# Weights alone in one DMA queue, x in five pieces issued by ScalarE, first chunk in three passes

## The reference, cut to what matters

```
def even_layer(h, norm_g, w_in, ...):
    p = rms_norm(h, norm_g) @ w_in
    ...
    return jnp.concatenate([o_a, o_b, o_m], axis=-1) @ w_out

def reference(x, mem, ...):
    h = x
    for layer in range(DEPTH):
        h = h + (even_layer if layer % 2 == 0 else odd_layer)(h, ...)
    return h
```

## Time and profile before

| | |
|---|---|
| median of 3 runs | 1442.42 us (1442.23 to 1443.27) |
| the profiled execution | 1443.31 us |
| its span in the profile | 1441.6 us |
| TensorE busy | 98% of the span |
| VectorE, ScalarE, GpSimd busy | 62%, 53%, 9% |
| bytes moved | 236.42 MB, 164 GB/s over the span |

### The profile page before, as it was taken

One profiled execution on the slowest core, in us unless ns is written; L12 is line 12 of the kernel. 1 busy time (PEld: TensorE's weight loads), 2 busy tenths in 40 slices (PEclk: granted clock), 3 DMA queues, 4 the chain that ended last, 5 costly groups with the idle time before them and its releaser, 6 DMA issues.

```text
span 1441.6 us, 18169 instructions
## 1 busy us (share of the span) xinstructions
PE 1413.8 (98%) x6869; PEld 1174.9 (82%) x6869; DVE 890.5 (62%) x1289; ACT 759.6 (53%) x1179; POOL 125.3 (9%) x126
## 2 busy tenths in 40 slices
PE   6999999999999999999999999999999999999998
PEld 5888789888789888878888788878878878887886
DVE  4447597777777788765566553654554645556563
ACT  4545532455532664666444545765755746765441
POOL 3001222010222010000000120020020020000000
PEclk9999999999999999999999999999999999999999
DMA  8555533455443476446455565455465564553562
GB/s 268 179 176 161 161 118 103 130 163 159 134 120 99 141 263 210 144 131 223 146 160 176 175 205 178 141 177 176 160 185 166 172 192 150 186 167 109 188 194 73
DMA packets 124847, 236.42 MB, mean 164 GB/s; under 512 B 9648, under 2 KB 10073, under 8 KB 124761
## 3 DMA queue, kind: packets, MB, share of 16 engines
q1 hardware_dynamic: 122585, 231.07, 51.2%
q10 hardware_dynamic: 2176, 4.19, 0.9%
HBM read 233.14 MB, written 2.10 MB: 163 GB/s over the span
## 4 chain that ended last, share of the span: by engine, by line
PE 90%; DVE 3%; POOL 2%; ACT 2%; issue 1%; SPq 1%; DMA 0%; DVEq 0%; ACTq 0%
PE job L1466 25%; PE job L1468 25%; PE job L1467 25%; PE mixer L1486 4%; PE mixer L1588 2%; PE mixer L1604 1%; PE mixer L1603 1%; DVE wlo L1137 1%; PE mixer L1718 1%; POOL proj L783 1%; PE mixer L1698 1%; POOL brs L725 1%; PE mixer L1576 1%; DVE reg L1211 1%; PE mixer L1568 0%
## 5 line engine op out<-in xcount | busy, mean ns | idle before, releaser
L1466 PE MATMUL job<-whi,xhi 128*128 128x512 f32 x1728 | 695.1, 402 | 0.3 <-DVE wlo L1137 0.3
L1137 DVE TENSOR_TENSOR wlo<-raw,whi 128x1024 fp32r<-128x1024 f32 x432 | 523.9, 1230 | 257.7 <-ACT whi L808 255.3
L1468 PE MATMUL job<-whi,xlo 128*128 128x512 f32 x1728 | 676.0, 391 | 0.0
L1467 PE MATMUL job<-wlo,xhi 128*128 128x512 f32 x1728 | 674.4, 390 | 0.0
L808 ACT ACTIVATE whi<-raw 128x1024 fp32r<-128x1024 f32 x432 | 445.4, 1056 | 136.5 <-PE job L1468 128.1
L1468 PEld LDWEIGHTS job<-whi,xlo 128*128 128x128 f32 x1728 | 325.0, 188 | 70.4
L1466 PEld LDWEIGHTS job<-whi,xhi 128*128 128x128 f32 x1728 | 325.8, 189 | 63.7 <-issue 0.7
L1467 PEld LDWEIGHTS job<-wlo,xhi 128*128 128x128 f32 x1728 | 326.2, 189 | 62.6
L1336 DVE SCALAR_TENSOR_TENSOR cvr<-cvr,vt 128x255 f32<-128x255 f32 (+14 forms) x240 | 118.2, 552 | 0.0
L835 ACT ACTIVATE proj<-job,rstd 128x512 f32<-128x512 f32 x80 | 50.5, 687 | 43.0 <-PE job L1468 35.5
L939 ACT ACTIVATE reg<-mixer 128x512 f32<-128x512 f32 x24 | 14.4, 599 | 92.4 <-PE mixer L1588 92.4
(11 more groups left out here) (245 smaller groups left out, 973.4 us busy)
## 6 DMA issues: line engine op xcount, KB each, us to landing
raw<-in_od_w_in_dram SPq DMA_DIRECT2D x160, 512.0 KB, 4.4
raw<-in_ev_w_in_dram SPq DMA_DIRECT2D x144, 512.0 KB, 3.8
raw<-in_ev_w_out_dram SPq DMA_DIRECT2D x48, 512.0 KB, 4.5
raw<-in_od_w_out_dram SPq DMA_DIRECT2D x48, 512.0 KB, 4.6
raw<-in_w_mem_kv_dram SPq DMA_DIRECT2D x32, 512.0 KB, 4.2
hid<-in_x_dram SPq DMA_DIRECT2D x4, 512.0 KB, 7.6
reg<-in_mem_dram ACTq DMA_DIRECT2D x4, 512.0 KB, 5.5
hid<-in_x_dram ACTq DMA_DIRECT2D x4, 512.0 KB, 7.5
```

The lines of the kernel that those rows point to most:

```text
L1137: vec.tensor_tensor(wlo[:, c % RING, :, :], raw[:, c % RAWS, :, :], whi[:, c % RING, :, :].bitcast(F32), ALU.subtract).then_inc(s_lo, 1)
L1466: mm(out_, xh, hi, start=first, stop=False)
L1467: mm(out_, xh, lo, start=False, stop=False)
L1468: return mm(out_, xl, hi, start=False, stop=last)
```

## The change

SP's queue keeps the chunk loads alone, from chunk 0 on. The gain row, x, the vector rows, `wba`, `alog` and `dtb` are issued by ScalarE, in the program ahead of its first activation, the copy of the gains. x comes in five pieces, two of 256 columns and three of 512. Split 0 moves to the front of its position in the plan, ahead of `xt` 0. `vec` moves from position 4 to position 6, which is behind chunk 5 and ahead of `rstd`. Chunk 0 is multiplied in three passes over its four (block, half) pairs: high by high, then high by remainder, then remainder by high, with waits of its own. TensorE multiplies the identity by itself six times into `mixer3` after the transpose of the gain row.

```
-FIRST = 4
+X_PIECES = ((0, 256), (256, 512), (512, 1024), (1024, 1536), (1536, 2048))
+WARM = 6
...
-        stream(7 if c < 16 else 0, max(-1, c - min(AHEAD, 2 + c // 4)), [(("split", c), 0)])
+        stream(-2 if c == 0 else 7 if c < 16 else 0, max(-1, c - min(AHEAD, 2 + c // 4)), [(("split", c), 0)])
...
-    stream(0, 4, [(("vec", 0), 0)])
+    stream(0, 6, [(("vec", 0), 0)])
...
-            sources = vecs(vrow)
-            sp.dma_start(sources[0][0], sources[0][1]).then_inc(s_gain, 16)
-            for b in range(FIRST):
-                sp.dma_start(hid[:, :, 512 * b:512 * b + 512],
-                             x[:, 512 * b:512 * b + 512].rearrange("(t p) d -> p t d", p=128)).then_inc(s_xin[b], 16)
-                load_chunk(b)
-            for dst, src in sources[1:]:
-                sp.dma_start(dst, src).then_inc(s_vrow, 16)
-            sp.dma_start(wba, w["ev_in"][:, BA0:BA0 + 16].rearrange("(k p) n -> p k n", p=128),
-                         allow_slow_non_contiguous=True).then_inc(s_small, 16)
-            sp.dma_start(alog[:, :], a_log.partition_broadcast(128)).then_inc(s_small, 16)
-            sp.dma_start(dtb[:, :], dt_bias.partition_broadcast(128)).then_inc(s_small, 16)
-            for c in range(FIRST, nch):
+            for c in range(nch):
                 load_chunk(c)
...
+            sources = vecs(vrow)
+            sc.dma_start(sources[0][0], sources[0][1]).then_inc(s_gain, 16)
+            for b, (c0, c1) in enumerate(X_PIECES):
+                sc.dma_start(hid[:, :, c0:c1], x[:, c0:c1].rearrange("(t p) d -> p t d", p=128)).then_inc(s_xin[b], 16)
+            for dst, src in sources[1:]:
+                sc.dma_start(dst, src).then_inc(s_vrow, 16)
+            sc.dma_start(wba, w["ev_in"][:, BA0:BA0 + 16].rearrange("(k p) n -> p k n", p=128),
+                         allow_slow_non_contiguous=True).then_inc(s_small, 16)
+            sc.dma_start(alog[:, :], a_log.partition_broadcast(128)).then_inc(s_small, 16)
+            sc.dma_start(dtb[:, :], dt_bias.partition_broadcast(128)).then_inc(s_small, 16)
             sc.wait_ge(s_vp, 1)
             act(vt[:, 0:16], M[0][:, 0:16], ACT.Copy).then_inc(s_vt, 1)
...
+            def first_chunk():
+                pe.wait_ge(s_hi, 1)
+                for k in range(2):
+                    pe.wait_ge(s_xh, k + 1)
+                    for t in range(T):
+                        mm(pj[0][t][:, :], xhi[:, SLOT[k], 128 * t:128 * t + 128], whi[:, 0, k, :], start=(k == 0), stop=False)
+                pe.wait_ge(s_lo, 1)
+                for k in range(2):
+                    for t in range(T):
+                        mm(pj[0][t][:, :], xhi[:, SLOT[k], 128 * t:128 * t + 128], wlo[:, 0, k, :], start=False, stop=False)
+                pe.wait_ge(s_xl, 2)
+                for k in range(2):
+                    for t in range(T):
+                        ins = mm(pj[0][t][:, :], xlo[:, SLOT[k], 128 * t:128 * t + 128], whi[:, 0, k, :], start=False, stop=False)
+                ins.then_inc(s_pe, 1)
...
+                if c == 0:
+                    first_chunk()
+                    return
...
-                    pe.wait_ge(s_xin[k // 4], 16)
+                    pe.wait_ge(s_xin[k // 2 if k < 4 else k // 4 + 1], 16)
...
             nc.tensor.transpose(M[0][:, 0:16], vrow[0:16, 0, :], ident[0:16, 0:16]).then_inc(s_vp, 1)
+            for _ in range(WARM):
+                mm(M[3][:, 0:128], ident[:, :], ident[:, :], start=True, stop=True)
```

More of the change, by code:

```diff
@@ L393, in prog @@
         s_small = sem("small_inputs_loaded")
-        s_xin = [sem(f"x_columns_loaded{b}") for b in range(4)]
+        s_xin = [sem(f"x_columns_loaded{b}") for b in range(len(X_PIECES))]
         s_min = sem("mem_loaded")
@@ L853, in do_rstd @@
                 if src == 0:
-                    for b in range(4):
+                    for b in range(len(X_PIECES)):
                         sc.wait_ge(s_xin[b], 16)
```

## The result

The changed kernel takes 1451.45 us (median of 4 runs, 1451.16 to 1451.64), the kernel before 1442.41 us (4 runs): the ratio is 1.0061, with a 95% interval of 1.0044 to 1.0079. The forecast was 1445.4 us in a range of 1441.5 to 1448.5. The sign was right, the size was not: +9.0 us by the medians, +7.8 us by the spans of the two profiled executions (1449.4 and 1441.6 us). The two differ because the profiled execution lay 0.9 us above the median before and 0.3 us under it after.

A forecast was written before the change was run, and what follows sets the result against it. TensorE, busy 98% of the span, was taken as the bound. Later work shifts by T + 21.1 + 0.4 - 35.11, which is T - 13.6 = +3.0 us, giving a median of 1445.4 us, range 1441.5 to 1448.5.

The forecast's parts named there:

- T: Moment when ScalarE, done with its issues, table load and `vt` copy, can begin `whi` of chunk 0: 16.6 us.
- `wba`, `alog` and `dtb`: Last three issues ahead of ScalarE's first activation, in the sum for T: 4.51 us, taken from SP's rows.
- The upper bound: T if ScalarE's first six issues and SP's six chunk issues exclude each other: 19.0 us.
- rival 2: Issues on ScalarE's queue pay less: T 14.7 us, +1.1 us, down to 11.6, -2.0 us, without `alog`'s wait; chance 0.25.
- half of `alog`'s wait: Low end of the forecast range, rival 2 with half of `alog`'s issue wait: 1441.5 us.
- table load, `vt` copy, gaps: Behind ScalarE's issues, now on the path to T: table load 1.28 us, `vt` copy 0.18 us.
- T to chunk 0: Split 0, two `xlo` and transposes between T and the first chunk 0 matmul: 3.6 us.
- chunk 0 to chunk 5: TensorE without a hole: chunk 0 with transposes 4.70 us, then four chunks at 3.21 us each.
- the hole before chunk 4: TensorE busy only 1.85 of 5.70 us between 24.30 and 30.00 us, as chunk 4 is issued late; predicted to go.
- Rival 1: Issues of the SP and ScalarE queues exclude each other: T 19.0 us, +5.4 us, 1447.8 us; chance 0.22.
- Rival 3: ScalarE's activations run beside its issues: T near 5.7 us, -7.9 us, 1434.5 us; chance 0.07.
- Rival 4: Chunk 4 is late for another reason, so the hole stays: near +10 us; chance 0.02.

The follow-up runs named there:

- number 5: Changed kernel without identity products, three passes and later `vec`, split 0 still in front: 1450.68 us.
- number 6: Changed kernel with `wba` loaded by four issues of 512 short runs instead of one of 2048: 1450.26 us (one run).
- number 2: Changed kernel with `wba`, `alog` and `dtb` issued right behind the gain row, ahead of x and the vector rows: 1451.29 us (one run).
- number 1: Changed kernel with `alog` and `dtb` issued ahead of `wba` instead of behind it: 1445.32 us, ratio 1.0012 to the kernel before.
- number 4: Kernel before with the fourteen rows, `wba`, `alog` and `dtb` issued by SP behind chunk 5 instead of chunk 3: 1441.84 us, ratio 0.999.
- number 3: Changed kernel with the fourteen rows, `wba`, `alog` and `dtb` on SP behind chunk 5; ScalarE issues only gain row and x: 1440.49 us, ratio 0.998.
- number 8: Number 7 plus identity multiplications where TensorE waits at the start: 1436.04 us, ratio 0.9952 to the kernel before.
- number 7: Kernel before with rows on SP behind chunk 5, and `alog`, `dtb`, `wba` issued by ScalarE at split 5: 1437.50 us, ratio 0.9963.
- number 10: Changed kernel, chunks 2 on held until x landed, rows behind chunk 5, `alog`, `dtb`, `wba` at split 5, identity products in four places: 1438.09 us, ratio 0.9964.

## Why the prediction was wrong in size

**The failed step** is the sum for T, where it says: "`wba`, `alog` and `dtb` 16.83 - 12.32 = 4.51 us". These three took 18.65 - 9.91 = 8.74 us. The term was a wait, read as a duration and carried to the other engine. In the kernel before, `alog`'s issue ended at 12.76 + 3.54 = 16.30 us, and that is when the last bulk load ahead of it landed (chunk 3, issued at 5.33 us, landed 11.0 us later; the split that waited for it began at 16.31 us). On ScalarE's queue the bulk ahead is x, and x shares the DMA engines with six chunks instead of four; it lands at 17.8 us, and the issue ends at 18.13 us. The prediction had put the landing of x and the six chunks at about 16 us and called it no limit; through this wait it was the limit. The upper bound kept the same 4.51 us, so it could not hold the time. The lower bound of rival 2, with 0.44 us for `alog`, had the right idea (the wait depends on what fills the queue) and the wrong sign; for the first vector row, whose issue fell from 1.37 to 0.54 us, it was right. Two slips moved nothing: the issues on ScalarE are 23, not 22 (the sum has all of them), and half of `alog`'s wait gives 1442.0 us, not 1441.5.

The other terms, in microseconds:

| term | forecast | measured |
|---|---|---|
| end of the gain row's and x's issues | 4.3 | 4.31 |
| fourteen rows | 6.30 | 5.58 (4.33 to 9.91) |
| `wba`, `alog`, `dtb` | 4.51 | 8.74 |
| table load, `vt` copy, gaps | 1.5 | 1.51 |
| T | 16.6 | 20.16 |
| T to chunk 0 | 3.6 | 3.68 |
| chunk 0 to chunk 5 | 17.5 | 18.10 |
| `vec` | 0.4 | 0.29 |
| wait at `ba` | none | 0.85 |

So T is late by 3.6 us, chunk 0 costs 0.6 more because the slow pitch lasted longer (its first eight matmuls came every 0.44 us and the last four every 0.35, where before seven were slow; 29.15 - 23.84 = 5.31 us with the transposes, forecast 4.70), and the wait at `ba` adds 0.85: 3.0 + 3.6 + 0.6 + 0.85 - 0.1 = 7.9 us, against 7.8 us between the spans. The wait at `ba` goes with the moved `vec` (number 5 has neither): ScalarE comes to the squares of x at 46.59 us, 9.7 us later than in the kernel before (36.85 us), where TensorE is only 7 us late, and splits `wba` behind them.

**What was right.** That ScalarE's issues hold all of the start (the wait of 13.70 us), that the table load comes onto the path, that the hole before chunk 4 goes and TensorE then runs on but for the 0.85 us, that three passes and identity products earn nothing here (number 5).

**Rival 1, issues that exclude each other,** came nearer to the result than the forecast, by luck: as priced, with whole issues that exclude each other, it is refuted. SP's six chunk issues and ScalarE's first six issues ran side by side:

```profile
0.81 3.41 SPq L664 DMA_DIRECT2D raw<-in_ev_w_in_dram  x6
```

Twelve issues were done by 4.31 us, 3.5 us in all; nine on one queue took 5.21 us before. An issue took 0.57 us on the one queue and 0.58 us on the other, against 0.58 us before, so no wait of one for the other shows. The Trainium skill (Perfetto Trace Analysis, "DMA Instruction — HWDGE (DVE, Sync)") says that the generator is locked for exclusive use while an issue makes its descriptors. If the lock lasted for most of an issue, the two queues would have had to share that time, and this trace does not agree. A lock held for a small part of each issue is not excluded.

**Rival 3,** activations beside the issues, is refuted by the first activation at 18.65 us. **Rival 4,** the hole kept, is refuted by the begins of chunks 4 and 5, 38.74 and 41.94 us, with no wait between; its +10 us stood as near to the measured 7.8 as rival 1's +5.4, by luck as well.

What stays open: how many pieces a queue holds. Number 6 shows that it is pieces that count, and number 2 that `wba` alone, with 2048, is enough for a wait; there `alog`'s issue ended at 7.50 us, well before `wba` had landed (1.30 + 11.4 us), so the room is neither zero nor all of them. That count was not measured, nor is it explained why issues of 1.1 to 1.3 us show in numbers 1 and 4 with no `wba` ahead. Putting the table load ahead of the issues was not tried.

## What to carry to other kernels

The duration of a DMA issue can be a wait for room in its queue: look at what ends with it, and when it moves, price what it waits for in the new place, not the microseconds of the old row. Issue a load of many short runs last on its queue, or where nothing stands behind it. Price every issue that is put ahead of an engine's first activation if other engines wait for that activation: 23 of them cost 17.8 us of ScalarE's time here, six cost 3.5 us and left the kernel faster than before (number 3). Products that only keep the clock up paid where they filled the waits up to the work and ended before its data was there (number 8); 13.7 us ahead of it they gained nothing.

## What was not expected of the hardware

The issue of `alog`, one small broadcast, lasted 0.40 us in numbers 7, 8 and 10 and 0.51 in number 1, where no `wba` stood ahead of it; 0.60 in number 6, where `wba`'s own four issues had done the waiting; and 2.53, 3.54, 4.52, 5.71, 7.73, 7.82 and 8.16 us in the other seven kernels. Two queues do not slow each other's issues much (twelve in 3.5 us), but they do slow each other's landings: x's first piece, half the size, was used at 7.57 us with six chunks on the other queue (number 3) and at 5.70 us in the kernel before, where x stood ahead of the chunks in one queue.
